# A two-block network on one core: the context's expert visits dealt a tenth more densely, and a tile's query and key scores computed in halves of 64 tokens

## The reference, cut to what matters

```
def chunk(hc):                                   # 128 tokens
    q = (hc @ w_query).reshape(PEER_CHUNK, PEER_HEADS, 2, D_KEY // 2)
    s = jnp.einsum('chpd,hpnd->chpn', q, sub_keys)
    s_top, i_top = lax.top_k(s, PEER_TOPK)       # 16 of 128 keys, twice per head
    ...
    best, pos = lax.top_k(cand, PEER_TOPK)       # 16 experts per head
    gate = jax.nn.softmax(best, axis=-1)
    u = jnp.take(u_tab, eid, axis=0)
    act = jax.nn.gelu(jnp.einsum('chkd,cd->chk', u, hc)) * gate
    v = jnp.take(v_tab, eid, axis=0)
    return jnp.einsum('chk,chkd->cd', act, v)
```

## Time and profile before

| | |
|---|---|
| median of 3 runs | 3284.21 us |
| profiled execution | 3281.02 us, span 3279.3 us |
| PE busy | 2348.2 us (72%) |
| PE weight loads busy | 1356.8 us (41%) |
| DVE busy | 1692.5 us (52%) |
| ACT busy | 577.9 us (18%) |
| POOL busy | 1481.8 us (45%) |
| DMA | 1097.74 MB, 335 GB/s on average |
| two gathers of a table, POOL | 768 each, 942 and 945 ns |
| dots, DVE | 768, 1222 ns each |

### The profile page before, as it was taken

The page is one execution under the profiler, slowest core; times in us unless marked ns, Lnnn a source line. Parts: engine busy times, 40 slices in busy tenths (PEclk is TensorE's granted clock), DMA queues, the critical chain, the costliest instruction groups (busy, mean ns, idle before and its releaser), DMA issues.

```text
span 3279.3 us, 40034 instructions
## 1 busy us (share of the span) xinstructions
PE 2348.2 (72%) x13944; PEld 1356.8 (41%) x13944; DVE 1692.5 (52%) x4471; ACT 577.9 (18%) x1213; POOL 1481.8 (45%) x1577
## 2 busy tenths in 40 slices
PE   6899957899899888885775754445997765544444
PEld 5477724466676554762540300002587452100000
DVE  2521576554333577347559554443724647744444
ACT  2320231411100235111111400001331111100000
POOL 1100035444444444434547577773000556777775
PEclk9999978799999897996875755556898886555555
DMA  8958579899999986997999999995245999999998
GB/s 310 356 185 297 204 265 349 318 355 361 368 364 370 349 320 240 372 398 282 402 395 397 350 403 409 409 409 215 73 161 199 366 402 360 393 409 409 409 409 348
DMA packets 351015, 1097.74 MB, mean 335 GB/s; under 512 B 27936, under 2 KB 39264, under 8 KB 350816
## 3 DMA queue, kind: packets, MB, share of 16 engines
q0 software_dynamic: 240192, 880.90, 69.9%
q1 hardware_dynamic: 110624, 214.29, 18.2%
HBM read 1094.03 MB, written 1.05 MB: 334 GB/s over the span
## 4 chain that ended last, share of the span: by engine, by line
PE 44%; DVE 18%; DMA 14%; issue 12%; PEld 6%; ACT 3%; POOL 1%; PEldq 1%; DVEq 0%; ACTq 0%; POOLq 0%
PE ps L446 18%; PE ps L482 11%; DVE UV L1174 8%; DMA UV<-in_v_tab,idxT 8%; PE ps L468 4%; PE ps L669 3%; PEld ps L669 3%; DMA W<-in_w_out 3%; PEld ps L446 3%; ACT arena L1894 2%; PE ps L438 2%; DMA W<-in_w_mod 2%; DMA W<-in_w_in 1%; PE ps L613 1%; PE ps L571 1%
## 5 line engine op out<-in xcount | busy, mean ns | idle before, releaser
L1174 DVE SCALAR_TENSOR_TENSOR UV<-ps,UV 128x1024 f32<-128x1024 f32 x768 | 909.8, 1222 | 816.3 <-PE ps L468 798.6
L2448 POOL DMA_INDIRECT UV<-in_u_tab,idxT x768 | 723.8, 942 | 1156.5 <-DVE UV L1174 613.3
L482 PE MATMUL ps<-UV,acts 128*32 128x512 f32 x3072 | 607.1, 873 | 486.5 <-DVE acts L1183 341.2
L2458 POOL DMA_INDIRECT UV<-in_v_tab,idxT x768 | 725.6, 945 | 266.7 <-issue 200.9
L446 PE MATMUL ps<-H,W 128*128 128x256 f32 (+2 forms) x2528 | 503.2, 361 | 32.4 <-ACT H L1894 25.9
L446 PEld LDWEIGHTS ps<-H,W 128*128 128x128 f32 (+1 forms) x2528 | 435.3, 199 | 117.6 <-issue 66.2
L468 PE MATMUL ps<-hs,selb 32*128 32x512 bf16 x1536 | 203.1, 515 | 200.8 <-DVE UV L1174 194.3
L482 PEld LDWEIGHTS ps<-UV,acts 128*32 128x32 f32 x3072 | 76.4, 127 | 634.9 <-DVE acts L1183 436.1
L468 PEld LDWEIGHTS ps<-hs,selb 32*128 32x128 bf16 x1536 | 42.0, 96 | 595.5 <-issue 329.1
L1894 ACT ACTIVATE gel<-dots 128x2 f32<-128x2 f32 x384 | 77.2, 202 | 1152.9 <-DVE UV L1174 1141.4
L446 PE MATMUL ps<-arena,W 128*128 128x256 f32 (+1 forms) x1120 | 254.3, 384 | 11.8 <-issue 4.8
(11 more groups left out here) (228 smaller groups left out, 1948.5 us busy)
## 6 DMA issues: line engine op xcount, KB each, us to landing
W<-in_w_in SPq DMA_DIRECT2D x42, 2048.0 KB, 14.3
UV<-in_w_mod POOLq DMA_DIRECT2D x18, 2048.0 KB, 12.4
W<-in_w_ff SPq DMA_DIRECT2D x16, 2048.0 KB, 14.2
W<-in_w_out SPq DMA_DIRECT2D x12, 2048.0 KB, 13.9
W<-in_w_query SPq DMA_DIRECT2D x10, 2048.0 KB, 19.5
UV<-in_w_ada POOLq DMA_DIRECT2D x9, 2048.0 KB, 11.8
W<-in_w_mod POOLq DMA_DIRECT2D x6, 2048.0 KB, 20.1
UV<-in_u_tab,idxT POOLq DMA_INDIRECT x768, 8.1
```

The lines of the kernel that those rows point to most:

```text
L482: last = mm(ps[q:q + GROUP, YB, :], acts[:, tok % SLOTS, GROUP - 1 - r:2 * GROUP - 1 - r], Vs[:, tok % SLOTS, hf * 512:(hf + 1) * 512], st ...
L1174: dve.scalar_tensor_tensor(out=Us[:, j, :], in0=ps[:, b:b + 2, :].rearrange("p a b -> p (a b)"), scalar=1.0, in1=Us[:, j, :], op0=MUL, op1 ...
L2448: pool.indirect_dma_start(Us[:, j, :], None, A["u_tab"], off).then_inc(sem(f"u_arrived{j}"), 16)
L2458: pool.indirect_dma_start(Vs[:, j, :], None, A["v_tab"], off).then_inc(sem(f"v_arrived{j}"), 16)
```

## The change: what it does, and the diff

Two things are changed.

First, `beat` takes a pace of 6.2 in place of 6.8 while fewer than 128 visits have been dealt, which is until the last pair of the context. From visit 128 on the pace is the old one. Before, visits 117 to 119 stood in `back_tile` and 120 to 127 in `route_first("x0")`; now the last context visit, 127, stands behind the ninth of the twelve pieces (`br`, 4) that carry them in tile 2's merge, and neither `back_tile` nor `route_first("x0")` has any. The eleven visits are spread over what comes before: one more in the routing of tile 1, one in the first block's products, one in its attention, two in its merge, three in its FFN, one in the norms around its end, one in `x0`'s front and one in `x0`'s attention. In `x0`'s merge there are nine as before. From visit 128 on nothing is dealt differently.

Second, in `route_first("x0")` and `route_first("x1")` the query of 128 tokens is replaced by four half queries of 64 tokens: heads 0 to 3 and 4 to 7 of the first 64 tokens, then the same of the second 64, each followed by its scores. The 32 weight blocks of each query are multiplied twice, each time with 64 token columns. Both weight tiles stay in the ring until the second half has used them.

```diff
+PACE_CTX = 6.2
...
-                while owed[0] >= PACE and seen[0] < min(segment[1], ready[0]):
-                    owed[0] -= PACE
+                pace = PACE_CTX if seen[0] < 2 * PAIRS else PACE
+                while owed[0] >= pace and seen[0] < min(segment[1], ready[0]):
+                    owed[0] -= pace
...
+            def query_half(tag, n, u, r, first=False):
+
+                w = weights(("wq", tag, n % 2, u))
+                o, at = bank(("wq", n, u, r)), n % 2 * P + HALF * r
+                for e in range(4):
+                    last = feature(o[:, e * HALF:(e + 1) * HALF], w, e * P, H, DT, first=first and e == 0, c=slice(at, at + HALF))
+                full(last, ("wq", n, u, r))
+                if r:
+                    done_with_weights()
+
+            def scores_half(n, u, r):
+
+                pe.wait_ge(sem("query_ready"), queries_before(n) + 2 * r + u + 1)
+                o = [bank(("sc", n, u, r, p)) for p in range(2)]
+                for i in range(2):
+                    for b in range(2):
+                        h, at = 4 * u + 2 * b + i, HALF * r
+                        for p in range(2):
+                            last = mm(o[p][HALF * b:HALF * b + HALF, i * P:(i + 1) * P], QP[n % 2][64 * p:64 * p + 64, h, at:at + HALF],
+                                      keys[64 * p:64 * p + 64, h, :], start=True, stop=True)
...
             def route_first(tag):
 
                 n = TILE_OF[tag]
-                for u in range(2):
+                for u in range(2 if tag == "c0" else 0):
                     query(tag, n, u, first=(u == 0))
                     beat(("wq", n, u), 7.0)
...
+                for i in range(4 if tag != "c0" else 0):
+                    r, u = i // 2, i % 2
+                    query_half(tag, n, u, r, first=(i == 0))
+                    beat(("wq", n, u, r), 4.0)
+                    if i == 0:
+                        pe.wait_ge(sem("keys_loaded"), nxt("keys_loaded", 16))
+                    scores_half(n, u, r)
...
-                    dve.wait_ge(sem("scores_ready"), 4 * n + 2 * (e // 2 + 1 if parts(n) == 1 else e + 1))
+                    dve.wait_ge(sem("scores_ready"), 2 * queries_before(n) + 2 * (e // 2 + 1 if parts(n) == 1 else 2 * r + e + 1))
...
+                for i in range(4 if tag != "c0" else 0):
+                    query_half(n, i % 2, i // 2)
+                    scores_half(n, i % 2, i // 2)
```

More of the change, by code:

```diff
@@ L46, in part_no, with queries_before @@
     return sum(parts(m) for m in range(n)) + r
+def queries_before(n):
+    return sum(2 * parts(m) for m in range(n))
 def steps_of(n):
@@ L515, in beat @@
                     seen[0] += 1
[L516 removed]
+                owed[0] = min(owed[0], pace)
             def stream(key, upto):
@@ L912, in scores @@
             def scores(n, a):
-                pe.wait_ge(sem("query_ready"), 4 * (n // 2) + 2 * (n % 2) + a + 1)
+                pe.wait_ge(sem("query_ready"), queries_before(n) + a + 1)
                 o = [bank(("sc", n, a, p)) for p in range(2)]
-                for hh in range(4 if parts(n) == 1 else 0):
+                for hh in range(4):
                     h = 4 * a + hh
@@ L922, in scores @@
                             full(last, ("sc", n, a, p))
-                for i in range(4 if parts(n) == 2 else 0):
-                    for b in range(2):
-                        h, at = 4 * a + 2 * b + i % 2, i // 2 * HALF
-                        for p in range(2):
-                            last = mm(o[p][HALF * b:HALF * b + HALF, i * P:(i + 1) * P], QP[n % 2][64 * p:64 * p + 64, h, at:at + HALF],
-                                      keys[64 * p:64 * p + 64, h, :], start=True, stop=True)
-                            if (i, b) == (3, 1):
-                                full(last, ("sc", n, a, p))
                 beat(("sc", n, a), 2.0)
@@ L1736, in route_first @@
                 n = TILE_OF[tag]
-                for u in range(2):
+                for u in range(2 if tag == "c0" else 0):
                     beat("wq", n, u)
                     beat("sc", n, u)
+                for i in range(4 if tag != "c0" else 0):
+                    beat("wq", n, i % 2, i // 2)
                 for u in range(2 if tag == "c0" else 0):
```

23 lines of the change are left out of this document (17 added, 6 removed).

## The result

Four runs gave 3367.81 us in the median (3363.26 to 3369.42) for the changed kernel and 3282.76 us (3279.72 to 3287.22) for the kernel before beside them: a ratio of 1.0262 [1.0245, 1.028], slower by some 85 us. The forecast was 3307 us with a range up to 3323. The profiled execution took 3363.26 us with a span of 3361.5, 82.2 us more than the span before.

A forecast was written before the change was run, and what follows sets the result against it. DMA was taken to bound the dense visits and PE the FFN; -34.1 + 33.4 + 23.1 = +22.4 us on 3281.0 gives 3303.4, with the median 3.2 above it 3306.6, say 3307 us; range 3280 to 3323.

The forecast's parts named there:

- Part 3: First routings of `x0` and `x1`: half queries take 7.2 us each, like whole ones, delaying the turned experts, together +23.1 us.
- groups that aren't at the full clock all through: Upper bound of the halves' cost: four groups of 64 records partly below full clock add 7.0 us per tile.
- the path through z0, the ranks and "keys 0": Routing of `x1`: z0 starts 15.3 us later, ACT spreads key ranks later, DVE's "keys 0" waits, turned experts come 11.1 later.
- Parts 1 and 2: Eleven visits leaving `x0`'s out products and routing save 34.1 us; dealt earlier they cost 33.4; the dealing alone -0.7.
- a doubled place: Two visits behind one piece: the second waits for DVE's dots and costs 3.3 us; the FFN's three more cost 9.9.
- (a): DMA bounds the added visits in the first block's products, merge and FFN, 5.15 us each: +11.9, 3319 us; chance 0.17.
- (b): The eleven added visits cost only PE's time, 1.4 us each, 15.4 in place of 33.4: +4.4, 3289 us; chance 0.15.
- (c): Half price: a half query takes 3.6 us, turned experts come 2.4 us sooner per tile: -5.5, 3279 us; chance 0.13.
- (d): The dealing doesn't do what it says; excluded by the order of instructions, no visit being left in `x0`'s first routing.
- a different clock in the routing: Part of "something else", with a weight load that comes late; to both sides of the forecast; chance 0.05.
- the band of 3298 to 3316: Program time for the sum as worked out, by its own bounds; chance 0.50.
- the signs named ahead: New profile: half query's 64 loads in 7.2 us; `x1` routing about 61 us, DVE idle some 13 before "keys 0"; `x0` about 62.

The follow-up runs named there:

- run 3: Changed kernel, each of the four half queries multiplying all 128 columns, ACT copying the wanted half: 3311.53 us, 1.0102 of the kernel before.
- run 4: Changed kernel, only the first of the four groups multiplying all 128 columns, the others 64: 3314.75 us, 1.0110 of the kernel before.
- run 10: Changed kernel with z0 moved ahead of the half queries, repeated beside the unaltered changed kernel: 3296.16 us, 1.0051 of the kernel before.
- run 1: Kernel before with the denser dealing alone (pace 6.2), queries whole: 3282.78 us against 3278.73, ratio 1.0011.
- run 9: Changed kernel again, unaltered: 3364.35 us against 3281.07 for the kernel before, ratio 1.0251.
- run 2: Changed kernel with the old pace of 6.8, so the half queries alone: 3349.69 us, 1.0230 of the kernel before.
- run 5: Changed kernel with z0 moved ahead of the half queries, on the chip with slow gathers: 1.0015 of the kernel before.
- run 7: Kernel before with the denser dealing, whole queries and z0 ahead of them, on the chip with slow gathers: 1.0007 of the kernel before.

## Why the prediction was wrong

The sign was right, and so was the path by which the halves reach the end of the program. The price of a half query was not: it hangs on TensorE's clock, which the sum had nowhere, and that one term was wrong by more than all the others together.

**Part 3, "a half query takes 7.2 us, like a whole one".** This is the step that failed. It was read from one-column products and a whole query, whose loads both followed each other at 111 to 112 ns, as they do at the full clock. What it left out is in which state of the clock a half query starts and whether it gets out of it. The whole query of before started low too: 10.20 us with a granted clock of 0.71 in the mean, against 7.3 and 7.4 for z0 and z1. The prediction used that row only for the end of the first query, and for its upper bound took another group that began low (9.13 us, at 0.80 in the mean). Runs 3, 4 and 10 show that the term is right when the clock is up (7.33 to 7.36 us), and the result shows 13.9 when it isn't. The bound of 7.0 us per tile for "groups that aren't at the full clock all through" supposed that each group would come up again as a 128-column group does; what came was four groups wholly at 0.50.

The sizes, from the profiled executions: in `x1` the stretch to the turned experts is 61.0 us with the clock up (run 3) and 88.0 with it down; forecast 61.2. In `x0` 63.5 and 90.3; forecast 62.1. So with the clock up the path through z0, the ranks and "keys 0", the wait for a bank and the gaps came out right to 1.4 us. Some of that is luck: the first group of run 3 ends 14.9 us after the norm's start where 15.9 were taken, and from group to group it is 8.6 us where 8.4 were. The clock adds 27.0 + 26.8 = 53.8. It can be counted in `x0`: four groups at 13.9 us instead of one at 8.9 and three at 7.4 make 24.5, four sets of scores at 1.13 instead of 0.67 make 1.8, the transposes the rest.

The Trainium skill (TensorE: Matmul & The Clock Gate, Part 1: The HAM clock gate) says that the throttled state is the default and that TensorE's own sustained activity releases it. By that rule the four halves, with PE busy but for 0.6 to 0.7 us between them, would have come up as the whole query did, and the loss would have been about run 3's. The trace doesn't agree for these products: 0.50 in all four. The measurement decides.

The rule cited ahead of the result, from the same page (LDWEIGHTS), that a load of 128 columns takes 107 ns whatever is multiplied, holds to some 6 ns in the runs at the full clock (7.22 us of loads in run 4, 113 ns each) and not in the changed kernel, with 215 ns at 0.50.

**Parts 1 and 2, the dealing, "about nothing (-0.7)".** Right in the sum: 0.0 at `x0`'s turned experts in run 1's profile, +4.1 us in the timed medians (1.0011 [1.0000, 1.0022]). Part by part, run 1 against before:

| stretch | forecast | run 1 |
|---|---|---|
| up to the first block's attention | +6.5 | +14.8 |
| from there to `x0`'s attention | +23.8 | +23.3 |
| from there to the norm | -2.2 | -8.0 |
| norm to turned experts | -28.8 | -30.1 |

The prices of a doubled place and of the FFN were good. The one visit in tile 1's routing was mis-sized, 12 us for 3.2. Two errors of 8 and 6 us cancelled, which is luck, and a profile can't tell such a sum to better than a few us: in five profiles of kernels that are the same up to `x0`'s norm (runs 1, 3, 4, 9 and the changed one) it starts anywhere from 1462.5 to 1467.1. What the sum missed altogether is that the dealing and the halves interact: the visits that leave `x0`'s routing would have raised the clock after the second half (run 2). That is 13.3 us (41.5 - 28.2), a part of the 26.8 above. It holds in the profiles; the timed runs (1.0230 alone, 1.0262 together) can't tell it from nothing.

**The rivals.** (a), DMA as the bound of the added visits, is out: the stretch from the first block's attention to `x0`'s grew by 23.3 us in run 1, where (a)'s own prices make it some 34. Its sign, PE waiting for v rows, is there in part: 7.5 us in run 1 between 840 and 1126 us, where the FFN before had none and 5.5 stood just ahead of it. (b), visits at PE's bare price, is out by the same number, since its eight visits would make 11.2 us, and by PE's wait for DVE at the doubled places. (c), half price, is out: 7.36 us, not 3.6. (d) was excluded already. What decided was the rest of 0.05, "a different clock in the routing". It deserved more: the query of 10.20 us was at hand, and no row showed that products with 64 columns bring the clock up as those with 128 do. Nor does the band of 3298 to 3316, which was given 0.50, follow from the terms' bounds: the upper one of part 3 alone, 7.0 us per tile, makes 3321 of 3307.

**What would show it.** Of the signs named ahead, DVE's wait for the ranks before "keys 0" and a longer routing in `x1` came true, with 28.7 us for 13 and 88.0 for 61; 64 loads in 7.2 us did not.

**The sum by what was measured** (the dealing with the changed kernel's norm and run 1's routing): the dealing, 34.7 at the norm less 30.1 in the routing, +4.6; the halves at the full clock, 63.5 - 48.8 = 14.7 in `x0` and 61.0 - 50.1 = 10.9 in `x1`; the clock, 53.8; between and behind the routings -1.8. Together +82.2 us, the difference of the spans.

**Left open.** What lets the clock fall isn't settled. It isn't only the wait of 4.0 us: in run 2's `x0` the longest wait ahead of the first half was 2.54 us. After a wait of 2.2 us alone it goes both ways. z1 of `x0`, behind 2.17 us, takes 9.01 us at 0.81 in the changed kernel and in run 3, and this in run 1:

```profile
1499.47 7.38 PE L671 MATMUL ps<-H,W 128*128 128x128 f32 x64 [2.17 <-ACTq L1902]
```

z0, which then has the 2.2 us wait and the norm's products ahead of it, took 7.31 us in five of six routings (runs 5, 7 and 10). No run takes away only the wait ahead of a half query, without other work in its place. Nor was another width than 64 and 128 tried at the low level. Why 64 columns don't raise the clock stays open too; the runs show only that they didn't, in all five routings whose halves began low with no visit between them (both of the changed kernel, both of run 9, and `x1` of run 2).

## What to carry to other kernels

Work out a group of products at both levels of the clock, and ask at which level it is entered: after a wait of PE, a group may stay at the low one for as long as it lasts, so that halving the columns nearly doubles its time (7.4 to 13.9 us here) in place of saving some. When a product's form changes behind such a wait, put other full-width work into the wait, as z0 here, which took 68 of 83 us back. And visits or other pieces that are moved away from a chain may have been what brought its clock up, as in run 2.

## What the runs showed of the hardware

- 64 float32 records with a weight load each take 7.31 to 7.41 us at a granted clock of 1.00, with 64 and with 128 columns, and 13.9 us at 0.50 with 64 columns.
- After waits of 2.2 and 4.0 us, 128-column products had the clock back within their first group (8.9 to 10.2 us) in the kernel before and in runs 1, 3 and 4; 64-column products kept 0.50 through 256 records in 61 us, with gaps of 0.6 to 0.7 us between groups, and kept 1.00 when they were entered at it.
- When the clock falls, the listed value doesn't always show it in the wait: the 4.0 us wait ahead of `x1`'s first group is listed at 0.50 in the kernel before and in runs 2 and 9, and at 0.99 and 1.00 in the changed kernel and run 4. In all of them the products behind it began at the low level.
- A visit's products of 512 columns, themselves slow (0.61 and 1.94 us for 0.40 and 1.06), were followed by scores and a half query at the full clock in run 2 (0.67 and 7.36 us).
- Chips differ in their gathers: 5.88 us a visit in the dense stretches on one and 5.15 on another, and the kernel before takes 3520.85 us on the one and 3279 to 3283 on the others.
